# Four small edits in the mixers of a two-layer encoder: a ring slot handed back one product later, a value tile in another PSUM bank, one copy moved from ScalarE to VectorE, and a value tile parted differently

## The reference

```python
u = rms_norm(h, norm_mix[l]); proj = u @ w_in[l]
q_a, f_a, i_a, g_a, b_b, c_b, h_b, c_q, c_kv, k_pe = jnp.split(proj, split_at, axis=-1)
o_a = hgrn2_mixer(q_a, f_a, i_a, g_a, lbs[l], hgrn_norm[l])      # gated linear recurrence in chunks of 64
o_b = short_conv_mixer(b_b, c_b, h_b, conv_w[l], conv_norm[l])   # width-3 causal convolution
o_c = mla_mixer(c_q, c_kv, k_pe, cos, sin, ...)                  # latent attention, 8 heads
h = h + concatenate([o_a, o_b, o_c]) @ w_out[l]
h = h + cross_attention(rms_norm(h, norm_cross[l]), rms_norm(mem, norm_mem[l]), wq, wk, wv, wo)
h = h + hier_moe(rms_norm(h, norm_ffn[l]), ...)                  # 32 experts, top-2 inside the top-1 group
```

## Time and profile before

| | |
|---|---|
| median of 3 runs | 901.88 us (901.23 to 902.51) |
| the profiled execution | 902.04 us, of which the span from first to last instruction 900.2 us |
| PE busy | 843.3 us (94% of the span), 5188 matmul records |
| DVE, ACT busy | 275.1 us (31%), 169.4 us (19%) |
| mean granted TensorE clock | 0.987 |
| read from HBM | 270.76 MB, 302 GB/s over the span |
| PE's waits for expert weights (L801) | 17.5 and 15.3 us, 9 times each |

### The profile page before, as it was taken

One profiled execution on the slowest core, in us unless ns is written; L12 is line 12 of the kernel. 1 busy time (PEld: TensorE's weight loads), 2 busy tenths in 40 slices (PEclk: granted clock), 3 DMA queues, 4 the chain that ended last, 5 costly groups with the idle time before them and its releaser, 6 DMA issues.

```text
span 900.2 us, 12111 instructions
## 1 busy us (share of the span) xinstructions
PE 843.3 (94%) x5188; PEld 564.8 (63%) x5188; DVE 275.1 (31%) x571; ACT 169.4 (19%) x399; POOL 15.0 (2%) x21
## 2 busy tenths in 40 slices
PE   8999999999999999989879999999999999877776
PEld 7888876679755655535527887766975644332333
DVE  2317557132234111101104674723122421110112
ACT  1211134411222000000012112451121200000003
POOL 0600000000000000000000000000000000000000
PEclk9999999999999999999999999999999999999899
DMA  9943555074678999999999445507766899999995
GB/s 348 390 171 132 188 187 187 12 302 162 272 283 339 427 424 429 426 428 425 426 422 380 150 156 194 204 1 272 312 280 226 341 428 424 428 427 427 427 422 234
DMA packets 25944, 272.64 MB, mean 303 GB/s; under 512 B 3232, under 2 KB 3616, under 8 KB 7200
## 3 DMA queue, kind: packets, MB, share of 16 engines
q1 hardware_dynamic: 24592, 270.52, 74.0%
q10 hardware_dynamic: 1296, 1.30, 0.5%
HBM read 270.76 MB, written 1.05 MB: 302 GB/s over the span
## 4 chain that ended last, share of the span: by engine, by line
PE 75%; DMA 20%; ACT 1%; SPq 1%; DVE 1%; issue 1%; another core or an unknown queue 0%; PEld 0%; DVEq 0%; PEldq 0%; ACTq 0%
DMA early<-in_expert_units 19%; PE bank L663 18%; PE bank L745 12%; PE bank L801 7%; PE bank L1165 6%; PE bank L775 4%; PE bank L841 3%; PE bank L722 3%; PE bank L853 3%; PE bank L730 2%; PE bank L1195 2%; PE bank L1176 2%; PE bank L984 2%; SPq L552 1%; PE bank L937 1%; PE bank L684 1%
## 5 line engine op out<-in xcount | busy, mean ns | idle before, releaser
L663 PE MATMUL bank<-uT,ring 128*128 128x256 f32 x480 | 107.0, 381 | 1.4 <-DVE uT L1786 0.8
L663 PEld LDWEIGHTS bank<-uT,ring 128*128 128x128 f32 x480 | 90.3, 190 | 15.2 <-issue 1.4
L801 PE MATMUL bank<-ring,xT 128*32 128x512 f32 x560 | 69.1, 630 | 17.7 <-DMA ring<-in_expert_units 17.5
L801 PE MATMUL bank<-early,xT 128*32 128x512 f32 x464 | 55.1, 610 | 15.4 <-DMA early<-in_expert_units 15.3
L1165 PEld LDWEIGHTS bank<-uT,ring 128*128 128x128 f32 x512 | 57.8, 192 | 1.1 <-DVE uT L1786 0.5
L1165 PE MATMUL bank<-uT,ring 128*128 128x128 f32 x512 | 57.8, 275 | 0.0
L745 PE MATMUL bank<-ring,early 128*128 128x512 f32 x128 | 56.6, 592 | 0.0
L801 PEld LDWEIGHTS bank<-ring,xT 128*32 128x32 f32 x560 | 17.5, 113 | 61.4 <-issue 43.9
L745 PE MATMUL bank<-ring,uT 128*128 128x512 f32 x128 | 55.9, 592 | 0.0
L853 PE MATMUL bank<-yy,states 128*128 128x512 f32 x112 | 54.1, 612 | 0.0
L2275 DVE TENSOR_TENSOR hid<-hid,bank 128x256 f32<-128x256 f32 x16 | 6.7, 421 | 150.1 <-ACT hid L1659 150.1
(11 more groups left out here) (328 smaller groups left out, 1034.0 us busy)
## 6 DMA issues: line engine op xcount, KB each, us to landing
ring<-in_expert_units SPq DMA_DIRECT2D x47, 2048.0 KB, 22.7
early<-in_expert_units SPq DMA_DIRECT2D x37, 2048.0 KB, 26.6
ring<-in_fixed_units SPq DMA_DIRECT2D x16, 2048.0 KB, 8.1
ring<-in_fixed_units SPq DMA_DIRECT2D x24, 1024.0 KB, 18.0
early<-in_expert_units SPq DMA_DIRECT2D x12, 1024.0 KB, 37.8
ring<-in_expert_units SPq DMA_DIRECT2D x8, 1024.0 KB, 6.3
early<-in_expert_units SPq DMA_DIRECT2D x8, 512.0 KB, 5.9
ring<-in_fixed_units SPq DMA_DIRECT2D x4, 512.0 KB, 5.3
```

Source lines behind the costliest of these rows:

```text
L663: mm = pe.matmul(o[row0:row0 + m], w[:, c, c0:c0 + m], rhs[:, c], start=(c == 0), stop=(c == chunks - 1))
L801: mm = pe.matmul(bank[2][32 * e:32 * e + 32, :], xT[:, 2 * n + c, 32 * e:32 * e + 32], w[:, e, :, c], start=(n == 0 and c == 0), stop=(n = ...
```

## The change

Four parts. (1) `free_unit("cq")` moves from ahead of the product `kv` to behind it, in both layers. (2) `ktok` is emptied by VectorE, behind its `kp_turned`, where ScalarE did it behind `lat_rstd`. (3) `xv3` takes bank 5 and its pieces are 3, 3 and 10 products; `mo0` and `mss1` take bank 3. (4) In layer 2's head `xv2` is made in pieces of 12, 2 and 2 products, the last behind `mix_xt3`, and its job stands behind `mix_xt3` in the list.

```diff
-              ("kv", "A", 6), ("kp", "V", 7), ("latss", "A", 0), ("ktok", "A", 1), ("o_in", "A", 2), ("ksum", "V", 3),
+              ("kv", "A", 6), ("kp", "V", 7), ("latss", "A", 0), ("ktok", "V", 1), ("o_in", "A", 2), ("ksum", "V", 3),
...
-              ("mo0", "A", 5), ("mo1", "A", 6), ("mss0", "A", 4), ("mss1", "A", 5), ("xv3", "A", 3),
+              ("mo0", "A", 3), ("mo1", "A", 6), ("mss0", "A", 4), ("mss1", "A", 3), ("xv3", "A", 5),
...
-JOBS += [(1, *job) for job in MIX_INPUTS[:3] + [("xv2", "A", 3)] + MIX_INPUTS[3:] + LAYER_JOBS[4:] + PLACES]
+JOBS += [(1, *job) for job in MIX_INPUTS + [("xv2", "A", 3)] + LAYER_JOBS[4:] + PLACES]
...
-                    part_of_values("xv2", v2, lay, 0, 13)
+                    part_of_values("xv2", v2, lay, 0, 12)
...
-                    part_of_values("xv2", v2, lay, 13, 2 * KC).then_inc(pe_job, 1)
+                    part_of_values("xv2", v2, lay, 12, 14)
                     transposes("mix", rows, 1, (1,))
+                    part_of_values("xv2", v2, lay, 14, 2 * KC).then_inc(pe_job, 1)
...
-                free_unit("cq")
                 wait_unit(base, "in_kv")
                 w = slot_view("in_kv")
                 o = begin("kv")
                 channel_tile(o[:, 0:S], w, 0, P, uT).then_inc(pe_job, 1)
+                free_unit("cq")
...
-                part_of_values("xv3", v3, lay, 0, 2)
+                part_of_values("xv3", v3, lay, 0, 3)
                 after("mt5")
...
-                part_of_values("xv3", v3, lay, 2, 6)
+                part_of_values("xv3", v3, lay, 3, 6)
...
-                copy_out("ktok", ktok.rearrange("p t c s -> p (t c s)"))
                 copy_out("o_in", flat(dl))
...
                 dve.sem_inc(M["kp_turned"], 1)
+                gone(dve.tensor_copy(ktok.rearrange("p t c s -> p (t c s)"), job("ktok")[:, :]))
```

## The result

The changed kernel takes 896.18 us (median of 8 runs, 894.04 to 898.76) against 901.15 us (median of 8 runs, 900.11 to 903.3) of the kernel before beside it: ratio 0.9944, 95% interval 0.9928 to 0.9960.

What follows compares the result with a forecast made beforehand. PE was taken to bound the kernel nearly everywhere, with DMA-bound expert streams following it; 1.12 + 0.50 + 1.60 + 0.86 = 4.08 us off 902.04 gave 897.96, a median of 897.8 us, range 896.8 to 900.1.

Steps and rivals of the forecast that it cites:

- What bounds the kernel: PE sets the pace nearly everywhere; expert weight streams are DMA-bound but start with PE, so mixer gains pass in full.
- Part 1: At `kv` behind `cq`, both layers: moving the slot's wait saves 0.56 us a layer, 1.12 in all; bounds 0.30 to 0.57.
- Part 2: At `u0` behind `ksum`, both layers: VectorE's copy saves 0.25 us a layer, 0.50 in all; bounds 0 to 0.32.
- Part 3: At `xv3` behind `mt2` to `mt5`: new bank and pieces save 0.80 us a layer, 1.60 in all; bounds 0.45 to 0.90.
- Part 4: Layer 2's head, at `f` behind `mix_xt3`: two products moved behind it save 0.86 us, once; bounds 0.60 to 0.95.
- The sum: All four savings together: 4.08 us off the profiled 902.04 us; 2.1 with all lower bounds, 4.5 with all upper.
- The range: 896.8 to 900.1 us: all upper bounds less 0.6 us for spread of runs, to all lower bounds plus 0.3.
- DMA kept nothing back: Rival at the expert weight streams: DMA keeps layer 1's 1.61 us, giving 899.4 us, or both layers', 901.0; chance 0.08.
- no new wait took the place of the old ones: Rival: new waits at `mq0`, `mss0` or ahead of `kp` give back up to 1.8 us; typically 899 us; chance 0.16.
- the move of bank and of slot: Rival: changing bank or slot does nothing; if `kv`'s late start were a change of weights' slot, 898.9 us; chance 0.04.
- the granted clock: Rival, slower: moved weight waits lower PE's clock in the expert quads; 8.2 us of it would eat the gain; chance 0.02.
- The layers' distance: Sign in the trace: the distance between the two layers, 431.1 us, shrinks by 2.5.

Runs made afterwards that it cites:

- delay_l1: The changed kernel with 46 further, overwritten products of 128 columns ahead of `kv` in layer 1: 907.05 us, ratio 1.0078 to the kernel before.
- delay_l2: The changed kernel with 46 further, overwritten products of 128 columns ahead of `kv` in layer 2: 906.06 us, ratio 1.0062 to the kernel before.
- padded: The changed kernel with idle products ahead of `kv`, 5 in layer 1 and 9 in layer 2: 900.18 us, ratio 0.9995 to the kernel before.
- p2_act_early: The kernel before with the turned keys' copy left on ScalarE but put ahead of the Exp for the latents' scale: 899.26 us, one run.
- p2_keys: The kernel before with only the turned keys' copy moved to VectorE, behind `kp_turned`: 900.09 us, ratio 0.9986.

## Why the prediction was right in its mechanism and wrong in its range

**What bounds the kernel: right.** PE sets the pace in the mixers, and a us there passes through the streams of weights. The streams start 1.45 and 1.44 us earlier behind `f`, as much as the mixers gained; the delays of 10.27 us in `delay_l1` and `delay_l2` come out at the end as 10.7 and 9.7. PE's waits for weights (L801) did not grow: 31.2 and 32.7 us in the changed kernel, 30.6 to 33.6 in the four profiles of the kernel before.

**Part 1: right.** 0.54 us a layer for 0.56. `kv` follows `cq` at the pitch, and the slot comes back at the same moment. 0.03 are lost again ahead of `kp`.

**Part 2: right in place, the term was mis-sized.** 0.12 us a layer for 0.25, since 0.20 of the 0.32 us gap stayed when the copy no longer stood in the way. The prediction named such a remainder, a change of shape, as the lower bound's reason and then took a value near the upper one. `mq0` was not caught by the latents, which were ready at 126.76, 0.30 us ahead of it.

**Part 3: right.** 0.79 us for 0.80; the 0.74 for the bank measured 0.64 by itself, because `mo0` then waits 0.15, and the third product gives that back. `mss0` stood 1.40 us behind the second piece: the thin cover held, with no wait.

**Part 4: right.** 0.86 us for 0.86, and VectorE ends last, at a cost of 0.08.

**The sum: 3.76 us by the traces for 4.08.** Of the missing 0.32 us 0.27 are part 2's.

**The range: wrong.** The step that failed is the one from the sum to the time: "the median should be 897.8", with 0.6 us for the spread of runs. The three runs of before had the median 901.88; the next five made it 901.15, and 101 runs have 900.7. From 901.88 to 901.15 is 0.73 us, and the forecast fell out of its range by 0.62: from the base of 901.15 the same bounds would have begun at 896.0 and held the 896.18. And 0.6 us was too little for a median of the changed kernel: single runs of the kernel before have a standard deviation of 1.2 us (898.2 to 905.3), and the profiles show where it is, outside the mixers, 1.07 us between executions, while the mixers repeat to 0.01. Three runs that lay within 1.3 us of each other had hidden that. As a ratio the forecast, 0.9955, lies inside both measured intervals. That the ratio fits so well is partly luck: the distances alone would give 0.9958, and the sum's overestimate of part 2 moved it toward the measured 0.9944 and 0.9952.

**What stays open.** The pooled means are 900.9 us (101 runs) and 896.5 (14 runs), 4.4 us apart with a standard error of 0.4. That is 0.65 more than 3.76. It isn't special to the whole change: of the eleven timed comparisons of an edited kernel with the kernel before, eight came out 0.6 to 1.3 us faster than their distances say and three 0.1 to 0.5 us slower, single parts and the whole alike, and the kernel before against itself came out 0.45 us faster. `padded` and the further profiles of the kernel before give no sign of a further cause, but they can't exclude one of half a us.

**The rivals.** DMA kept nothing back that the spread between executions would let one see; no new wait took the place of the old ones; the move of bank and of slot each did what it says; the granted clock had no further effect that the distances show. The layers' distance shrank by 2.47 us between the two first profiles, for the 2.5 forecast, but a second profile of the kernel before puts it 2.3 us higher, so that this sign proves little: by the distances 2.31 us of it are the change.

## What to carry to other kernels

Where an engine waits for its own last product only to hand a buffer back, put the next group of products (here the 16 records of `kv`) between: here the wait then cost nothing, and the buffer came back at the same moment. When a filler tile has to wait for its bank, change the bank first; here more filler behind that wait gave nothing until then. Judge edits of half a us by distances between places of one trace, and give a forecast of the absolute time the spread of many runs, not that of the three at hand.

## What the runs showed of the hardware

PE's instruction stream runs ahead of the array far enough that in the changed kernel `free_unit("cq")` behind 16 records of `kv` released SP 7.30 us behind the start of `cq`, to 0.01 us the same as directly behind `cq`. Directly behind it the wait for PE's own last product costs 0.57 us, although the profile lists 0.30.

Between `ksum` (records of 128x256) and `u0` (64x128) 0.20 us more than the pitch pass with no wait listed, whether the copy that `u0` reads ended 0.46, 0.60 or 0.86 us ahead of it (`p2_act_early`, the changed kernel, `p2_keys`).

The same program's start varied by 3.3 us: `f` of layer 1 at 59.47 in one profile of the kernel before and at 56.08 to 56.27 in three others.
